# Combining expert results: plain gathers and vector adds, or gathers that add into the residual in four lists

## The reference, cut to what matters

```python
h = rmsnorm(x, norm_ffn)
p_sel, g_sel = top_k(softmax(h @ w_group_router), 1)        # one group of 4 experts
top_v, top_i = top_k(expert scores inside that group, 2)    # two experts of it
dense_w[token, expert] = softmax(top_v) * p_sel             # zero for the 14 others
for e in range(16):
    he = silu(h @ w_gate_e[e]) * (h @ w_up_e[e])
    out = out + dense_w[:, e:e + 1] * (he @ w_down_e[e])
x = x + out
y = rmsnorm(x, norm_final)
```

## Time and profile before

| | |
|---|---|
| three runs | 1429.13, 1455.76 (median), 1459.41 us |
| profiled execution, span from first to last instruction | 1435.5 us |
| span below the median of the runs | 20.3 us |
| mean granted TensorE clock | 0.919 of full speed |
| PE / DVE / ACT / POOL busy | 1235.1 / 760.1 / 544.0 / 85.7 us |

### The profile page before, as it was taken

One profiled execution on the slowest core, in us unless ns is written; L12 is line 12 of the kernel. 1 busy time (PEld: TensorE's weight loads), 2 busy tenths in 40 slices (PEclk: granted clock), 3 DMA queues, 4 the chain that ended last, 5 costly groups with the idle time before them and its releaser, 6 DMA issues.

```text
span 1435.5 us, 18227 instructions
## 1 busy us (share of the span) xinstructions
PE 1235.1 (86%) x7830; PEld 1088.5 (76%) x7830; DVE 760.1 (53%) x893; ACT 544.0 (38%) x608; POOL 85.7 (6%) x162
## 2 busy tenths in 40 slices
PE   4998999999778789999999897899378889889860
PEld 3996678999766579999999895499356767767650
DVE  6123533661488752323335514423678787788745
ACT  5224542332211142222215323312246666667732
POOL 2000210000011100000000000000010000000003
PEclk8998999999777799999999999899589999999985
DMA  8231001222200012332426420001679999999815
GB/s 275 92 122 30 1 0 39 67 87 67 53 1 0 16 44 74 98 77 91 134 80 227 155 88 30 1 1 67 234 264 334 327 366 326 341 369 340 317 78 197
DMA packets 123844, 197.76 MB, mean 138 GB/s; under 512 B 4264, under 2 KB 71968, under 8 KB 123760
## 3 DMA queue, kind: packets, MB, share of 16 engines
q1 hardware_dynamic: 115200, 167.00, 34.9%
q0 software_dynamic: 6256, 21.16, 4.0%
q10 hardware_dynamic: 2304, 8.39, 1.4%
HBM read 177.89 MB, written 18.65 MB: 137 GB/s over the span
## 4 chain that ended last, share of the span: by engine, by line
PE 67%; DVE 18%; ACT 8%; issue 3%; DMA 2%; POOL 1%; ACTq 0%; DVEq 0%; POOLq 0%
PE ps L1693 42%; PE ps L772 7%; DVE buf_r L706 5%; ACT buf_r L699 4%; PE ps L762 4%; PE ps L1781 3%; DVE buf_r L402 2%; PE ps L1881 2%; DVE buf L1548 1%; DVE buf L1536 1%; PE ps L2008 1%; ACT buf L841 1%; PE ps L1759 1%; PE ps L1795 1%; DMA buf<-y_rows,buf 1%
## 5 line engine op out<-in xcount | busy, mean ns | idle before, releaser
L1693 PE MATMUL ps<-buf_r,buf_r 128*128 128x288 f32 (+1 forms) x4752 | 611.5, 291 | 8.4 <-DVE buf_r L402 7.0
L1693 PEld LDWEIGHTS ps<-buf_r,buf_r 128*128 128x128 f32 x4752 | 608.7, 189 | 9.6 <-DVE buf_r L402 7.6
L706 DVE TENSOR_TENSOR buf_r<-buf,buf_r 128x2048 fp32r<-128x2048 f32 x96 | 219.5, 2289 | 61.7 <-ACT buf_r L699 60.9
L392 DVE TENSOR_TENSOR buf_r<-buf,buf_r 128x2048 fp32r<-128x2048 f32 (+2 forms) x53 | 116.0, 2189 | 245.6 <-ACT buf_r L386 245.6
L699 ACT CAST buf_r<-buf 128x2048 fp32r<-128x2048 f32 x96 | 182.9, 1910 | 81.9 <-PE ps L772 38.2
L762 PE MATMUL ps<-buf_r,buf_r 128*128 128x512 f32 x768 | 186.3, 399 | 17.1 <-DVE buf_r L402 17.0
L762 PEld LDWEIGHTS ps<-buf_r,buf_r 128*128 128x128 f32 x768 | 143.9, 191 | 53.3 <-DVE buf_r L402 23.9
L386 ACT CAST buf_r<-buf 128x2048 fp32r<-128x2048 f32 (+2 forms) x53 | 96.6, 1822 | 150.3 <-PE ps L1693 150.3
L772 PE MATMUL ps<-buf_r,buf_r 128*128 128x512 f32 x384 | 97.6, 412 | 27.7 <-DVE buf_r L875 27.7
L772 PEld LDWEIGHTS ps<-buf_r,buf_r 128*128 128x128 f32 x384 | 74.1, 196 | 48.2 <-DVE buf_r L875 31.5
L398 ACT CAST buf_r<-buf 128x1024 fp32r<-128x1024 f32 (+4 forms) x52 | 45.7, 891 | 34.1 <-DVE buf L883 23.1
(11 more groups left out here) (276 smaller groups left out, 1132.6 us busy)
## 6 DMA issues: line engine op xcount, KB each, us to landing
buf<-in_w_gate_e SPq DMA_DIRECT2D x32, 1024.0 KB, 8.4
buf<-in_w_up_e SPq DMA_DIRECT2D x32, 1024.0 KB, 7.2
buf<-in_w_down_e SPq DMA_DIRECT2D x32, 1024.0 KB, 7.4
buf<-in_w_in SPq DMA_DIRECT2D x16, 1024.0 KB, 5.8
buf<-in_w_in SPq DMA_DIRECT2D x17, 512.0 KB, 5.1
buf<-in_w_mem_kv SPq DMA_DIRECT2D x8, 1024.0 KB, 5.6
y_rows<-buf ACTq DMA_DIRECT2D x16, 512.0 KB, 7.9
buf<-in_x_prompt SPq DMA_DIRECT2D x8, 512.0 KB, 4.9
```

The costliest lines, as they stand in the source:

```text
L392: nc.vector.tensor_tensor(r32(raw), raw, w_hi(n), ALU.subtract).then_inc(wl_ready, 1)
L706: nc.vector.tensor_tensor(e_lo(t), e_raw(t), e_hi(t), ALU.subtract).then_inc(wl_ready, 1)
L1693: last = nc.tensor.matmul(out, a, b, start=(k == 0 and j == 0), stop=(k == len(parts) - 1 and j == 2))
```

## The change

The table gets a row of zeros, row 0, and the expert results move up by one row. Routing makes four lists of rows in place of `R12`: for each token the row of its first expert if that is below 14 and else row 0 (`R_EARLY[:, 0]`), the same of its second expert (`R_EARLY[:, 1]`), the row of whichever of its two is expert 14 and else row 0 (`R_14`), and the same for expert 15 (`R_15`). `R_OVER` is for rows of overflow passes. Each list is applied to the five chunks of `X` by an indirect transfer that adds what it reads to its destination. POOL waits for all of a list to land before it issues the next, since two adds to the same bytes must not be in flight together. The DVE adds, the buffers `XG` in the combining and the two branches around the gathers go; ACT waits for the transfers of list 15 by itself.

```diff
-        y_rows = nc.dram_tensor("y_rows", [NE * CAP, D], F32, kind="Internal").ap()
+        y_rows = nc.dram_tensor("y_rows", [1 + NE * CAP, D], F32, kind="Internal").ap()
...
+        last_rows = [fin_loaded[0], fin_loaded[1], xg_loaded[1], xg_loaded[2], xg_loaded[3]]
+        last_count = [16, 16] + [16 * (NE // NXG) + 16] * 3
...
-                for s_, r, i in ((S1, R1F, 0), (S2, R2F, 1)):
+                for s_, i in ((S1, 0), (S2, 1)):
                     go(v.tensor_tensor(TMP, POSP, s_, ALU.mult))
-                    go(v.tensor_reduce(r, TMP, AX.X, ALU.add))
-                    go(v.tensor_copy(R12[:, i, :].bitcast(U32), r))
+                    go(v.tensor_reduce(ROWF[:, i, :], TMP, AX.X, ALU.add))
+                row14, row15, over = (float(1 + P * (NE - i)) for i in (2, 1, 0))
+                go(v.scalar_tensor_tensor(out=R_EARLY.bitcast(U32), in0=ROWF, scalar=row14, in1=ROWF,
+                                          op0=ALU.is_lt, op1=ALU.mult))
+                go(v.scalar_tensor_tensor(out=LATE, in0=ROWF, scalar=row14, in1=ROWF, op0=ALU.is_ge, op1=ALU.mult))
+                go(v.scalar_tensor_tensor(out=LAST, in0=LATE, scalar=row15, in1=LATE, op0=ALU.is_ge, op1=ALU.mult))
+                go(v.tensor_tensor(LATE, LATE, LAST, ALU.subtract))
+                go(v.tensor_tensor(R_14.bitcast(U32), LATE[:, 0, :], LATE[:, 1, :], ALU.add))
+                go(v.scalar_tensor_tensor(out=R_OVER.bitcast(U32), in0=LAST, scalar=over, in1=LAST, op0=ALU.is_ge, op1=ALU.mult))
+                go(v.scalar_tensor_tensor(out=LATE, in0=LAST, scalar=over, in1=LAST, op0=ALU.is_lt, op1=ALU.mult))
+                go(v.tensor_tensor(R_15.bitcast(U32), LATE[:, 0, :], LATE[:, 1, :], ALU.add))
...
-                act.dma_start(y_rows[e * P:(e + 1) * P, :], YO[e % 2]).then_inc(y_stored[e % 2], 16)
+                act.dma_start(y_rows[1 + e * P:1 + (e + 1) * P, :], YO[e % 2]).then_inc(y_stored[e % 2], 16)
...
+            pool.wait_ge(late_stored, 16 * 4)
+            pool.memset(XG[3][0:1, :], 0.0).then_inc(route_const, 1)
+            pool.wait_ge(route_const, 5)
+            out_dma(pool, y_rows[0:1, :], XG[3][0:1, :], late_stored)
+            pool.wait_ge(late_stored, 16 * 5)
             pool.wait_ge(idx_ready, 2)
             experts_pool(pool)
             pool.wait_ge(gt_psum, NE)
             pool.wait_ge(idx_ready, 3)
+            pool.wait_ge(late_stored, 16 * 5)
+            for i in range(2):
+                pool.wait_ge(y_stored[i], 16 * (NE // 2 - 1))
+            for m in range(NC_):
+                add_rows_of(pool, rows_below(NE - 2), R_EARLY[:, 0, m:m + 1], m, first_rows)
+            pool.wait_ge(first_rows, 16 * NC_)
+            for m in range(NC_):
+                add_rows_of(pool, rows_below(NE - 2), R_EARLY[:, 1, m:m + 1], m, second_rows)
+            pool.wait_ge(second_rows, 16 * NC_)
+            pool.wait_ge(y_stored[0], 16 * (NE // 2))
+            for m in range(NC_):
+                add_rows_of(pool, rows_below(NE - 1), R_14[:, m:m + 1], m, first_rows)
+            pool.wait_ge(first_rows, 32 * NC_)
             count = pool.value_load(FLAG[0:1, 1:2].bitcast(U32), min_val=0, max_val=T)
...
             for i in range(2):
                 pool.wait_ge(y_stored[i], 16 * (NE // 2))
-            with pool.If(count > P):
-                gather_results(pool, y_rows)
-            with pool.If(count <= P):
-                gather_results(pool, y_rows[0:NE * P, :])
+            for m in range(NC_):
+                add_rows_of(pool, rows_below(NE), R_15[:, m:m + 1], m, last_rows[m])
...
+        def rows_below(e):
+
+            return y_rows[0:1 + e * P, :]
+
+        def add_rows_of(pool, rows, index, m, done):
+
+            n = CH[m][1]
+            pool.indirect_dma_start(X[:n, m, :], None, rows, bass.IndirectOffsetOnAxis(ap=index.bitcast(U32)[:n, :], axis=0),
+                                    compute_op=ALU.add).then_inc(done, 16)
...
-                act.wait_ge(x3_ready, m + 1)
+                act.wait_ge(last_rows[m], last_count[m])
                 norm_stat(N_F + m, X[:n, m, :], n, SQ2)
...
-            for m, (_, n) in enumerate(CH):
-                dve.wait_ge(fin_loaded[m % 2], 32 * (m // 2 + 1))
-                nc.vector.tensor_tensor(X[:n, m, :], X[:n, m, :], XG[2 * (m % 2)][:n, :], ALU.add).then_inc(y1_sum, 1)
-                dve.wait_ge(y1_sum, m + 1)
-                nc.vector.tensor_tensor(X[:n, m, :], X[:n, m, :], XG[2 * (m % 2) + 1][:n, :], ALU.add).then_inc(x3_ready, 1)
-                if m:
-                    finish(m - 1)
-            finish(NC_ - 1)
+            for m in range(NC_):
+                finish(m)
...
-            sp.wait_ge(late_stored, 16 * (4 + NC_))
+            sp.wait_ge(late_stored, 16 * (5 + NC_))
```

More of the change, by code:

```diff
@@ L291, in encoder_step @@
         TMP, TMP2, DW, POSP, POSM = (A.view(NC_, NE) for _ in range(5))
-        R1F, R2F = A.view(NC_), A.view(NC_)
-        R12 = A.view(2, NC_)
+        ROWF, LATE, LAST = (A.view(2, NC_) for _ in range(3))
+        R_EARLY, R_OVER = A.view(2, NC_), A.view(2, NC_)
+        R_14, R_15 = A.view(NC_), A.view(NC_)
         GATE = A.view(NE)
@@ L453, in encoder_step @@
         fin_loaded = [sem(f"fin_loaded{i}") for i in range(2)]
-        y1_sum, x3_ready, fin_ready = (sem(n) for n in ("y1_sum", "x3_ready", "fin_ready"))
+        first_rows, second_rows, fin_ready = (sem(n) for n in ("first_rows", "second_rows", "fin_ready"))
+        last_rows = [fin_loaded[0], fin_loaded[1], xg_loaded[1], xg_loaded[2], xg_loaded[3]]
+        last_count = [16, 16] + [16 * (NE // NXG) + 16] * 3
         KV_STORES = 4
@@ L977, in overflow_act @@
             act.wait_ge(yo_ready, NE + nth(e, j))
-            act.dma_start(y_rows[bass.ds(e * P + NE * P * j, P), :], YO[0]).then_inc(y_stored[0], 16)
+            act.dma_start(y_rows[bass.ds(e * P + (NE * P * j + 1), P), :], YO[0]).then_inc(y_stored[0], 16)
         def moe_sp(sp):
@@ L991, in moe_pool @@
             pool.iota(IOTA, [[1, P]], base=0, channel_multiplier=0, allow_small_or_imprecise_dtypes=True).then_inc(route_const, 1)
[L992 removed]
+            pool.iota(ECAP, [[P, NE]], base=1, channel_multiplier=0, allow_small_or_imprecise_dtypes=True).then_inc(route_const, 1)
             for i in range(4):
@@ L1010, in moe_pool @@
                         pool.wait_ge(y_stored[0], 16 * (NE // 2) + nth(e, j, 16))
+                for i in range(2):
+                    for m in range(NC_):
+                        add_rows_of(pool, y_rows, R_OVER[:, i, m:m + 1], m, first_rows)
+                    pool.wait_ge(first_rows, 16 * NC_ * (3 + i))
             for i in range(2):
                 pool.wait_ge(y_stored[i], 16 * (NE // 2))
-            with pool.If(count > P):
-                gather_results(pool, y_rows)
-            with pool.If(count <= P):
-                gather_results(pool, y_rows[0:NE * P, :])
+            for m in range(NC_):
+                add_rows_of(pool, rows_below(NE), R_15[:, m:m + 1], m, last_rows[m])
             for m, (t0, n) in enumerate(CH):
```

## The result

The changed kernel is slower. Its median was 1452.68 us over 4 runs (1444.14 to 1460.41), beside 1446.59 for the kernel before (1429.13 to 1459.41, 4 runs). The ratio is **1.0124**, 95% interval 1.0078 to 1.0171. The first ratio is made from the runs in the quicker of two states, which leaves out 1455.76 and 1459.41 of the kernel before, so it is not the quotient of the two medians (1.0042). I had forecast a gain of 5 us. The predicted 1451 lies close to 1452.68 only because I measured the gain from a median that 4 runs did not keep.

What follows compares the result with a forecast made beforehand. Bound: waits among DMA, POOL and DVE after expert 15's store. 1366.3 + 18 x 2.3 + 4 x 2.4 + 1.0 + 2.0 = 1420.3; plus 8.8 + 1.4, span 1430.5, 5.0 under 1435.5; median 1451 us, range 1420 to 1479.

Steps and rivals of the forecast that it cites:

- start and landing of four lists: In the combining, each list pays 2.4 us uncovered: about 1.6 from POOL's issue to first bytes, 0.8 from last bytes to semaphore.
- other traffic in the chain: Last weight load and stores of experts 14 and 15 beside the lists: 4 us at full rate, 2 put on the chain.
- load of the count and branch: POOL's value load of the count ahead of the fourth list, 1.0 us, like the pause before the first gather.
- My sign for the bad side: In the profile after: a list takes over 14 us, or lists three and four take longer than one and two.
- c: DMA engines' time for one adding transfer of 128 rows in the combining: 1.9 to 2.6 us, taken as 2.3.
- the price of the four lists: Combining: from 1366.3, 18 transfers at 2.3 us, 4 x 2.4, 1.0 and 2.0 put the last landing at 1420.3 us.
- The reference time: Whole kernel: median of runs 1455.76 us, 20.3 above the profiled span of 1435.5; that difference was carried over unchanged.
- The slow zero row: Rival: lists three and four read row 0 for some 504 of 576 rows at half rate, adding 21 us: 1472; chance 0.10.
- POOL as the pace: Rival: POOL takes twice 0.94 us to write an adding transfer, pace 2.2 us, 1449 us again; chance 0.06.
- Hidden lists: Rival: reads and writes overlap, three lists end before expert 15's store lands; 16 us faster, 1440 us; chance 0.20.
- Adds that don't overlap inside an engine: Rival: an engine reads `X`, reads the source and writes in turn, 3.84 us a transfer; 23 us slower, 1479; chance 0.18.
- The small edits: Zero row's memset and store in POOL's idle time cost 0; six more small DVE instructions in `rows_step` cost 1.3 us.

## Why the prediction was wrong

The terms of the sum, in the changed kernel's profile:

| term | predicted us | measured us |
|---|---|---|
| expert 13's store to the first issue | 9.2 | 9.1 |
| 18 transfers of 128 rows | 18 x 2.3 = 41.4 | 18 x 2.7 = 48.6 |
| start and landing of four lists | 4 x 2.4 = 9.6 | 4 x 3.4 = 13.6 |
| other traffic in the chain | 2.0 | 6.0 |
| load of the count and branch | 1.0 | 2.1 |
| last landing to the end | 8.8 | about 10.2 |
| `rows_step` | 1.3 (taken as 1.4) | 1.3 |

The measured 2.7 is 0.52 MB at list three's 197 GB/s and also the middle of list four's landings, 3.4 is what list three's 15.5 us leave over 4.5 x 2.7, and 6.0 is by how much lists one and two are longer than list three. From the first issue to the last landing (list four's last issue at 1423.75 took 8.4 us to land, so 1432.2) it was 70.4 us and not 54.0.

**The mechanism was right and its sizes were not.** Each list waited for the one before, list three was the one in the way, and the fourth began long after expert 15's store. My sign for the bad side, a list of over 14 us, came with 15.5 to 19.3. My break-even stood at c = 2.6, and the forecast lay on the good side only because I took 2.3. Of the 16.4 us, 7.2 are c, 4.0 the gaps, 4.0 the other traffic and 1.1 the branch. With c alone at 2.7 my sum gives 1437.7, 2 us above the 1435.5 of the kernel before: c turned the sign. The terms beside it, 12.6 us in the sum and 21.7 measured, made most of the loss, with 1.4 more from the last landing to the end.

**The failed step is the price of the four lists, c first.** I set c between 1.9 (reads and writes share an engine) and 2.6 (the read side sets the pace) and chose the middle, with no row for it; it is 2.7. Its base was also too low: 1.28 us is 0.52 MB at 410 GB/s, the best slices of the earlier trace rows, where their mean is 363 GB/s, 1.44 us. The full slices of the adds are at 197 GB/s. By the rule that I cited from the Trainium skill, Collectives: The Full Stack, The bandwidth ceiling, an adding transfer needs two source reads and runs at 1/1.93 of the copying rate, which the page measured on collectives of four ranks; the slices come near it, with 363 / 197 = 1.85. My estimate by that page was 2.5, still short of 2.7; the same estimate on 1.44 us is 2.8. No run here looks inside an engine, so that the second read is what takes the time is the page's account, and the part of about a quarter that goes by rows and not by bytes isn't in it; shown are the rate and how it moves with the bytes.

**The second error was the overlap: with other traffic and in the gaps.** I wrote that the pauses between lists would take half of it. They didn't: POOL waits for a landing, and a landing waits for whatever shares the engines. List one took 19.3 us beside the end of the weight loads, 24.0 when it started earlier still. Start and landing were 3.4 us a list and not 2.4; what makes them 1 us longer the runs don't show. The run with one wait a chunk shows what these pauses are worth: 13 us or more, and with them gone the adding transfers lose nothing to the kernel before that the interval shows. What I said of the weights themselves held: the cast at the changed kernel's 1373.95 waited 0.47 us for ACT's own work, as in the earlier trace rows.

**The reference time.** I put 20.3 us between the profiled span and a run, the difference to a median of three. The results list both: 1444.14 us beside a span of 1442.4 for the changed kernel, and 1438.13 beside 1436.1 for an execution of the kernel before. Launch and end are about 2 us; the profiled execution simply was one of the quicker ones. This made 1451 look better than it was and doesn't touch the sign.

**The rivals.** The slow zero row: refuted. POOL as the pace: refuted at full rows; at half the bytes POOL and the engines are about even. Hidden lists: would have failed with plain gathers too, where list four was issued 12.2 us after expert 15's store and not 4.4. Adds that don't overlap inside an engine, c = 3.84: too dear, though its sign was the one that came.

**The small edits** came out as written: zero row in POOL's idle time, six small DVE instructions for 1.3 us of PE's waiting.

## What to carry to other kernels

Before work is started early in pieces, add up all the pieces: four lists that must not overlap, each rewriting the whole residual, cost more than the window that they were to fill, though each was cheap. Cut a job so that the early part is as much work as before and needs no filler; here that is one ordering of two indices (lower row first), and it was worth 1% with either kind of transfer. Where pieces must follow each other, wait for each part by itself: one wait a chunk in place of one a list took back the loss. When the sign of a forecast hangs on one unknown whose bounds hold the break-even, the middle between the bounds is no reason for either sign; weigh the ends.

## What the runs showed of the hardware that I had not expected

An adding indirect transfer occupies POOL 1.54 us and a plain one 0.94. In list one the issues stretch, to 3.35 us at the most. The full engines are not the reason: in list three they are as full and each issue of a full chunk takes 1.54. In all the profiles here an issue of over 1.6 us (1.0 for a plain one) runs for 0.7 us or more beside an instruction of DVE, and one with no DVE instruction beside it takes 1.42 to 1.60 (0.90 to 0.96); some beside DVE keep that time too. No run changes DVE's part alone, so that it is the reason is not shown. From the changed kernel's timeline:

```profile
1367.23 2.29 DVE L718 TENSOR_TENSOR buf_r<-buf,buf_r 128x2048 fp32r<-128x2048 f32 x1 [0.78 <-ACT buf_r L711]
1367.58 3.35 POOL L1062 DMA_INDIRECT buf<-y_rows,buf  x1 [0.30 <-issue]
```

A 0.5 MB store that lands in 3.0 us on idle queues took three times that beside adding transfers in flight, and 8.8 us beside plain gathers; the DMA issues of the changed kernel from 1386 to 1396 us (KB each, us to landing), with expert 15's store:

```profile
y_rows<-buf ACTq DMA_DIRECT2D x1, 512.0 KB, 9.7
```
